# Turning the residual stream of a two-layer decoder: tokens on partitions, 512-column moving weights, norms along rows

## The reference, cut to what matters

```python
for layer in range(2):
    mixer = even_mixer if layer == 0 else odd_mixer      # mLSTM + pooling, or gated linear attention
    x = x + mixer(rmsnorm(x, norm[layer]))               # ends in y @ w_out, w_out is (2048, 2048)
    h = rmsnorm(x, f_norm[layer])
    # product-key expert retrieval: 8 heads x 16 of 16384 one-neuron experts
    q = h @ w_q                                          # (2048, 2048), then scores, top-k, softmax g
    a = h . u_tab[expert]                                # first table, 16384 x 2048
    x = x + sum(g * gelu(a) * v_tab[expert])             # second table, 16384 x 2048
out = rmsnorm(x, final_norm)

def rmsnorm(x, g):
    return x * rsqrt(mean(x * x, axis=-1) + 1e-6) * g    # mean over the 2048 channels of a token
```

## Time and profile before

| | us |
|---|---|
| median of 3 runs | 4150.47 (4147.67 to 4150.59) |
| the profiled execution, its own time | 4150.45 |
| its span, first to last instruction | 4148.7 |
| PE busy | 4056.4 (98% of the span) |
| PE weight loads (PEld) busy | 3989.7 (96%) |
| DVE busy | 2624.9 (63%) |
| ACT busy | 1848.2 (45%) |
| POOL busy | 146.1 (4%) |
| mean granted TensorE clock | 0.989 of 2.4 GHz |
| DMA | 705.65 MB, mean 170 GB/s |

### The profile page before, as it was taken

The page is one execution under the profiler, slowest core; times in us unless marked ns, Lnnn a source line. Parts: engine busy times, 40 slices in busy tenths (PEclk is TensorE's granted clock), DMA queues, the critical chain, the costliest instruction groups (busy, mean ns, idle before and its releaser), DMA issues.

```text
span 4148.7 us, 90161 instructions
## 1 busy us (share of the span) xinstructions
PE 4056.4 (98%) x34860; PEld 3989.7 (96%) x34860; DVE 2624.9 (63%) x4001; ACT 1848.2 (45%) x2326; POOL 146.1 (4%) x142
## 2 busy tenths in 40 slices
PE   8999999999999999999899999999999999999998
PEld 7999999999999999999898889999999999999998
DVE  4555678778549955444545553887787479655444
ACT  4344444444544444444444444444444544444443
POOL 1111000000000000000003020000000000000000
PEclk9999999999999999999998999999999999999999
DMA  5455565655554555555543456556555654565554
GB/s 177 146 156 169 177 182 182 182 165 157 173 171 157 159 187 190 182 182 182 159 153 118 145 165 185 178 182 182 176 157 162 182 162 157 164 200 182 182 182 152
DMA packets 193647, 705.65 MB, mean 170 GB/s; under 512 B 21808, under 2 KB 22000, under 8 KB 193184
## 3 DMA queue, kind: packets, MB, share of 16 engines
q1 hardware_dynamic: 190224, 692.21, 54.3%
q0 software_dynamic: 3344, 12.32, 0.8%
HBM read 698.16 MB, written 6.29 MB: 170 GB/s over the span
## 4 chain that ended last, share of the span: by engine, by line
PE 92%; DVE 4%; DMA 2%; ACT 1%; issue 1%; POOL 0%; SPq 0%; DVEq 0%; POOLq 0%; ACTq 0%
PE ps L1422 29%; PE ps L1423 28%; PE ps L1424 28%; PE ps L1775 2%; DMA w_raw<-in_dense 1%; DVE w_lo L926 1%; DVE big L986 1%; DMA w_raw<-in_v_tab 1%; ACT w_hi L493 1%; PE ps L1683 0%; PE ps L1684 0%; PE ps L1685 0%; PE ps L1629 0%; DVE act_lo_t L975 0%; PE ps L1731 0%
## 5 line engine op out<-in xcount | busy, mean ns | idle before, releaser
L1422 PE MATMUL ps<-act_lo_t,w_hi 128*128 128x256 f32 x10112 | 2902.7, 287 | 46.2 <-DVE act_lo_t L975 35.3
L1423 PE MATMUL ps<-act_hi_t,w_lo 128*128 128x256 f32 x10112 | 2870.4, 284 | 0.0
L1424 PE MATMUL ps<-act_hi_t,w_hi 128*128 128x256 f32 x10112 | 2869.3, 284 | 0.0
L926 DVE TENSOR_TENSOR w_lo<-w_raw,w_hi 128x1024 fp32r<-128x1024 f32 x1312 | 1619.4, 1235 | 1392.6 <-ACT w_hi L493 1379.2
L493 ACT ACTIVATE w_hi<-w_raw 128x1024 fp32r<-128x1024 f32 x1312 | 1388.7, 1059 | 1727.5 <-DMA w_raw<-in_v_tab 888.7
L1422 PEld LDWEIGHTS ps<-act_lo_t,w_hi 128*128 128x128 f32 x10112 | 1948.4, 193 | 57.5 <-issue 40.3
L1423 PEld LDWEIGHTS ps<-act_hi_t,w_lo 128*128 128x128 f32 x10112 | 1950.7, 193 | 0.1
L1424 PEld LDWEIGHTS ps<-act_hi_t,w_hi 128*128 128x128 f32 x10112 | 1949.1, 193 | 0.0
L846 ACT ACTIVATE big<-ps 128x256 f32 (+1 forms) x256 | 98.6, 385 | 282.8 <-PE ps L1424 282.4
L1309 DVE TENSOR_TENSOR big<-big,ps 128x512 f32 (+1 forms) x128 | 171.2, 1339 | 8.4 <-PE ps L1775 8.4
L1369 DVE TENSOR_TENSOR act_lo_t<-big,act_hi_t 128x256 fp32r<-128x256 f32 x384 | 160.3, 419 | 0.0
(11 more groups left out here) (219 smaller groups left out, 1341.4 us busy)
## 6 DMA issues: line engine op xcount, KB each, us to landing
w_raw<-in_u SPq DMA_DIRECT2D x512, 512.0 KB, 3.5
w_raw<-in_v_tab SPq DMA_DIRECT2D x512, 512.0 KB, 3.7
w_raw<-in_dense SPq DMA_DIRECT2D x288, 512.0 KB, 3.6
x_spill<-big POOLq DMA_DIRECT2D x16, 256.0 KB, 4.8
big<-x_spill POOLq DMA_DIRECT2D x16, 256.0 KB, 4.5
big<-in_xT SPq DMA_DIRECT2D x4, 512.0 KB, 5.5
big<-in_keys POOLq DMA_DIRECT2D x2, 1024.0 KB, 11.1
out<-big SPq DMA_DIRECT2D x4, 512.0 KB, 2.7
```

What stands on the lines that cost most here:

```text
L926: dve.tensor_tensor(w_lo[:, slot, :], w_raw[:, slot, :], w_hi[:, slot, :].bitcast(F32), ALU.subtract).then_inc(s_lo, 1)
L1422: pe.matmul(out, wh, xl, start=start, stop=False, **kw)
L1423: pe.matmul(out, wl, xh, start=False, stop=False, **kw)
L1424: return pe.matmul(out, wh, xh, start=False, stop=stop, **kw)
```

## The change

The residual lies with tokens on partitions: two blocks (tb) of 128 tokens x 2048 channels. The output projections and the second table are computed in the form of the value projections (activation stationary, 512 weight columns moving). Of the host's layouts, `w_out` is cut by groups of 512 columns and `x`, the result and the last gain come by rows. A norm becomes: ACT squares a row piece with a sum along the row (`square`), DVE adds four sums, ACT the root, DVE the reciprocal (`deviation`); PE multiplies the residual by a diagonal matrix of these reciprocals, which turns it back to channels on partitions and scales it in one (`turn`); ACT and DVE make `act_hi_t` and `act_lo_t` from PSUM with the gain as scale (`turned_hi`, `turned_lo`). POOL adds the two parts to get `h` where the small gate projections need it (`whole`). The last slabs of `out` and `vt` are taken token block by token block, so that the first block's norm can start under the second's matmuls. The last norm needs no turning. `spread` reads PSUM with a step and writes runs of eight tokens.

```diff
+            def whole(fill):
+                for c in range(CHUNKS):
+                    pool.wait_ge(s_alo, KB * fill + 2 * c + 2)
+                    pool.tensor_tensor(at(HT + 512 * c, 512, 2), act_hi_t[:, 2 * c:2 * c + 2, :].bitcast(F32),
+                                       act_lo_t[:, 2 * c:2 * c + 2, :].bitcast(F32), ALU.add).then_inc(s_h, 1)
...
+                if layer == 1:
+                    pool.wait_ge(s_used, SLAB0["vt", 1] + 2 * HALF + RING)
+                    pool.dma_start(at(F_GAIN, D), last_gain).then_inc(s_last_gain, 16)
...
+            def square(k, n):
+                tb, c = ROWS[k][n]
+                if k == 0:
+                    act.wait_ge(s_x[2 * tb + c // 2], 16)
+                else:
+                    act.wait_ge(s_xadd, rows_added(k, n + 1))
+                i = 4 * tb + c
+                act.activation(at(HT + 512 * i, 512), xs(tb, c), ACT.Square,
+                               accum_out=ssq[:, i:i + 1]).then_inc(s_square, 1)
+            def deviation(k, tb):
+                act.wait_ge(s_msum, TB * k + tb + 1)
+                act.activation(root[:, tb:tb + 1], msum[:, tb:tb + 1], ACT.Sqrt, bias=epst[:, 0:1],
+                               scale=1.0 / D).then_inc(s_root, 1)
+            def deviations(k, n0=0):
+                for n in range(n0, FIRST_DONE[k]):
+                    square(k, n)
+                deviation(k, 0)
+                for n in range(FIRST_DONE[k], 8):
+                    square(k, n)
+                deviation(k, 1)
+            def turned_hi(k):
+                for j in range(KB):
+                    if j % 4 == 0:
+                        act.wait_ge(s_turned, TB * KB * k + KB + j + 4)
+                    act.activation(act_hi_t[:, j, :].rearrange("p (b t) -> p b t", b=TB), turned(j), ACT.Copy,
+                                   scale=gain[:, G_NORM[k] + j:G_NORM[k] + j + 1]).then_inc(s_ahi, 1)
+            def norm(k, n0):
+                hi(0, n0)
+                hi(1, n0 + 1)
+                turned_hi(k)
+                hi(2, n0 + 2)
+                hi(3, n0 + 3)
...
+                for s in range(RING, 32):
+                    lo(s % RING, n0 + s)
+                    if s % 8 == 3:
+                        g = s // 8 - 1
+                        dve.wait_ge(s_used, n0 + 8 * g + 8)
+                        for tb in range(TB):
+                            dve.tensor_tensor(xs(tb, g), xs(tb, g), bank(OUT_BANKS[layer][g % 2][tb]),
+                                              ALU.add).then_inc(s_xadd, 1)
+                k = 2 * layer + 1
+                for tb in range(TB):
+                    if tb == 0:
+                        dve.wait_ge(s_ypart, 4 * layer + 1)
+                    else:
+                        dve.wait_ge(s_used, n0 + 32)
+                    dve.tensor_tensor(xs(tb, 3), xs(tb, 3), bank(OUT_BANKS[layer][1][tb]), ALU.add).then_inc(s_xadd, 1)
+                    deviation(k, tb)
+            def deviation(k, tb):
+                dve.wait_ge(s_square, 8 * k + (8 if tb else FIRST_DONE[k]))
+                dve.tensor_reduce(msum[:, tb:tb + 1], ssq[:, 4 * tb:4 * tb + 4], AX.X, ALU.add).then_inc(s_msum, 1)
+                dve.wait_ge(s_root, TB * k + tb + 1)
+                ins = dve.reciprocal(rroot[:, tb:tb + 1], root[:, tb:tb + 1])
+                if k == 4:
+                    ins.then_inc(s_diag, 1)
+                else:
+                    chain(ins)
+                    dve.tensor_scalar(diag[:, tb, :], ident[:, :], rroot[:, tb:tb + 1], None, ALU.mult).then_inc(s_diag, 1)
+            def turned_lo(k, fill):
+                for j in range(KB):
+                    if j % 4 == 0:
+                        dve.wait_ge(s_ahi, KB * fill + j + 4)
+                    dve.scalar_tensor_tensor(out=act_lo_t[:, j, :].rearrange("p (b t) -> p b t", b=TB), in0=turned(j),
+                                             scalar=gain[:, G_NORM[k] + j:G_NORM[k] + j + 1],
+                                             in1=act_hi_t[:, j, :].bitcast(F32).rearrange("p (b t) -> p b t", b=TB),
+                                             op0=ALU.mult, op1=ALU.subtract).then_inc(s_alo, 1)
...
-                    grid = at(HALF * T * part, HALF * T).rearrange("p (e t) -> p t e", t=T)
+                    grid = at(HALF * T * part, HALF * T).rearrange("p (e t) -> p e t", t=T)
-                    dst = grid[:, t0:t0 + 8, :] if isinstance(i, int) else grid[:, bass.ds(t0, 8), :]
-                    dve.tensor_tensor(dst, dst, bank(4 + k, 512, 8), ALU.mult).then_inc(s_g, 1)
+                    dst = grid[:, :, t0:t0 + 8] if isinstance(i, int) else grid[:, :, bass.ds(t0, 8)]
+                    dve.tensor_tensor(dst, dst, bank(4 + k).rearrange("p (t e) -> p e t", t=8),
+                                      ALU.mult).then_inc(s_g, 1)
...
+                def add(n):
+                    tb, c = BY_BANK[n]
+                    if c < 2:
+                        dve.wait_ge(s_used, vbase + 2 * N_KEYS - RING)
+                    elif n < 7:
+                        dve.wait_ge(s_ypart, 4 * layer + 1 + (n - 4) + 1)
+                    else:
+                        dve.wait_ge(s_used, vbase + 2 * N_KEYS)
+                    dve.tensor_tensor(xs(tb, c), xs(tb, c), bank(2 * c + tb),
+                                      ALU.add).then_inc(s_xadd, 1)
+                for n in range(4):
+                    add(n)
+                if layer == 1:
+                    dve.wait_ge(s_last_gain, 16)
+                    dve.wait_ge(s_xadd, rows_added(k, 4))
+                    for c in range(2):
+                        dve.tensor_tensor(at(F_SCALED + 512 * c, 512), xs(1, c), at(F_GAIN + 512 * c, 512),
+                                          ALU.mult).then_inc(s_scaled, 1)
+                for n in range(4, 6):
+                    add(n)
+                deviation(k, 0)
+                def finished(tb, c):
+                    dve.scalar_tensor_tensor(out=at(F_OUT + D * tb + 512 * c, 512), in0=xs(tb, c),
+                                             scalar=rroot[:, tb:tb + 1], in1=at(F_GAIN + 512 * c, 512),
+                                             op0=ALU.mult, op1=ALU.mult).then_inc(s_fin, 1)
+                if layer == 1:
+                    dve.wait_ge(s_diag, TB * k + 1)
+                    finished(0, 0)
+                    finished(0, 1)
+                add(6)
+                add(7)
+                if layer == 1:
+                    finished(0, 2)
+                    finished(0, 3)
+                deviation(k, 1)
+                if layer == 1:
+                    dve.wait_ge(s_diag, TB * k + 2)
+                    finished(1, 2)
+                    finished(1, 3)
...
+            def turn(k):
+                for tb in range(TB):
+                    pe.wait_ge(s_diag, TB * k + tb + 1)
+                    for j in range(KB):
+                        pe.matmul(ps[:, j // 4 * 2 + tb, P * (j % 4):P * (j % 4 + 1)],
+                                  at(XT + D * tb + P * j, P), diag[:, tb, :], start=True, stop=True).then_inc(s_turned, 1)
+            def out_gemm(layer, beside):
+                n0 = SLAB0["out", layer]
+                def piece(g, q, tb):
+                    for k in range(2):
+                        kb = 2 * q + k
+                        if g == 0 and tb == 0:
+                            pe.wait_ge(s_alo, KB * FILL["y", layer] + kb + 1)
+                        c = slice(512 * k, 512 * (k + 1))
+                        t = slice(P * tb, P * (tb + 1))
+                        o = bank(OUT_BANKS[layer][g % 2][tb])
+                        pe.matmul(o, act_lo_t[:, kb, t], w_hi[:, q % 4, c], start=kb == 0, stop=False)
+                        pe.matmul(o, act_hi_t[:, kb, t], w_lo[:, q % 4, c], start=False, stop=False)
+                        ins = pe.matmul(o, act_hi_t[:, kb, t], w_hi[:, q % 4, c], start=False, stop=kb == KB - 1)
+                    return ins
+                for g in range(4):
+                    if g >= 2:
+                        pe.wait_ge(s_xadd, rows_added(2 * layer + 1, 2 * (g - 1)))
+                    for q in range(8 if g < 3 else 4):
+                        pe.wait_ge(s_lo, n0 + 8 * g + q + 1)
+                        piece(g, q, 0)
+                        piece(g, q, 1).then_inc(s_used, 1)
+                        if g == 0 and q in beside:
+                            beside[q]()
+                for q in range(4, 8):
+                    pe.wait_ge(s_lo, n0 + 24 + q + 1)
+                    ins = piece(3, q, 0)
+                ins.then_inc(s_ypart, 1)
+                for q in range(4, 8):
+                    piece(3, q, 1).then_inc(s_used, 1)
+                turn(2 * layer + 1)
...
+                    for tb in range(TB):
+                        for n in range(2):
+                            ins = v_piece(s, half, buf, tb, n)
                     ins.then_inc(s_used, 1)
+                def v_piece(s, half, buf, tb, n):
```

(24 more changed lines are left out.)

293 lines of the change are left out of this document (103 added, 190 removed).

## The result

| | before | after |
|---|---|---|
| median of 4 runs each | 4149.07 (4146.87 to 4150.59) | 4050.49 (4048.42 to 4051.30) |
| the profiled execution | 4150.45 | 4048.42 |
| its span | 4148.7 | 4046.7 |
| mean granted TensorE clock | 0.989 | 0.992 |

The ratio is 0.9767, with a 95% interval from 0.9755 to 0.9778: 98.6 us less by the medians, 102.0 by the two profiled executions, against 110 forecast. The time lies in the range given, 4028 to 4062.

The account below looks back on a forecast made before the run. The prediction took PE, busy 98% of the span, as the bound. Its terms 92 + 4 + 3 + 5 + 5 = 109 us less, rounded to 110, gave 4040 us from 4150.45, range 4028 to 4062.

Parts of the forecast that it names:

- matmul form, 576 slabs: Output projections and second table: a slab goes from 2.88 to 2.72 us, 92 us less.
- norms 1 and 3: After the output projections: 4.2 us saved, a new wait of 2.3 against it, 4 us less for both.
- norm 2: After the second table: 37.0 us become 33.6, with a PE wait of 6.4 us, 3 us less.
- the end: After the last table, to the span's end: 32.1 us become 27.0, 5 us less.
- the start: Program start: the second block begins at 32 instead of 37.08, 5 us less, between 4 and 7.
- layer 1's `out`, opening: One wait of about 6 us replaces several short ones; about even, up to 3 us either way.
- would take 3.16: Second-table slabs beside `scatter`: PE's time for a slab falls from 3.32 to 3.16 us.
- The ring: Supply of weight slabs: three slabs at the new pace are 8.16 us, leaving 1.7 us of slack of 2.2.
- `spread`: DVE beside `scatter`: 1.0 us taken, bounds 0.69 and twice the present length; rival that it becomes the bound, chance 0.03.
- the prediction's own formula: DVE beside `scatter` in the second table: with a `spread` of X us it needs 2.48 + X/2 a slab.
- the boundaries: Rival: the reordered norms, start and end give nothing or lose; 4058, up to 4068 us; chance 0.13.
- The 512 form: Rival: 512-column matmuls don't keep their pace in the table, the ring holding slabs at 2.88 us; 4123 us; chance 0.04.

Follow-up runs that it names:

- the tail experiments: Two runs, tail_staggered and tail_plain, that changed the order of the table's last four slabs in the changed kernel: 4041.49 and 4049.11 us.
- half_moving: The changed kernel with each 512-column matmul of the second table split into two of 256: 4116.36 us, ratio 0.9921 to the kernel before.
- no_low_part: The changed kernel without the second table's matmuls with `w_lo`, part of the computation missing: 3874.12 us, a single execution.
- tail_plain: The changed kernel with each table's last four slabs in the order of all others, no token block early: 4049.11 us, ratio 0.9766.
- combined: The changed kernel with tail_staggered's order, layer 1's `out` opening reordered on ScalarE and VectorE, and the last gain fetched in eight pieces: 4033.25 us, ratio 0.9723.
- before_warm: The kernel before, with 40 unread matmuls of ones put between the first norm's sum and the first projection: 4145.16 us, ratio 0.9997.
- tail_staggered: The changed kernel with each table's last four slabs begun as they arrive: 4041.49 us, ratio 0.9744 to the kernel before.

## Why the prediction was right, and where it was not

| step | forecast, us less | measured in the two profiles |
|---|---|---|
| matmul form, 576 slabs | 92 | 88: 448 x 0.16 + 128 x 0.127 |
| norms 1 and 3 | 4 | 3.7 |
| norm 2 | 3 | 2.9 |
| the end | 5 | 4.9 |
| the start | 5 | 8.2 |
| layer 1's `out`, opening | 0, up to 3 either way | -4.0 |

Norms 1 and 3 are 29.7 and 29.5 us before, 27.2 and 27.1 after, counted as in the table of the tail experiments, and 0.6 of each difference belongs to the form. The last row is layer 1's `out` up to its last four slabs, 90.0 us before and 89.5 after: 0.5 less, where the form alone takes off 28 x 0.16 = 4.5. The rows add to 103.7; four slabs each of norm 2 and the end are in two of them, 1.3 us, which leaves 102.4, against 102.0 between the two profiled executions. The forecast had the same double count. That it closes so well is partly chance. The tables' parts beside `scatter` are 19.4 us shorter, where the form gives 16.3, and the slabs between them and the last four 57.6 shorter, where it gives 60.2. Both have stalls that come and go: before, one slab at half clock at 1234 us (2.6 us) and one at 3572 (2.4); after, three of 0.75 beside the reload of x and the 2.0 behind the gain's transfer.

- **The matmul form** carried the forecast, and half_moving shows it for what it is: at the full clock 0.013 us for each matmul with its weight load, at 256 columns and at 512. The Trainium skill ("TensorE: Matmul & The Clock Gate", Back-to-back issue gap) gives 2.5 ns for the gap of an isolated matmul, by which the change would bring an estimated 17 us, and it says that beside weight loads this is too little for few columns and too much for 512. The trace does not agree: it has 13 ns at 512 columns too. The step that was off is "would take 3.16" beside `scatter`. The measured slab is 3.20, 4 us in all, and why the switch between the two forms of matmul takes 0.48 us now and took 0.45 is open.
- **The ring**: "1.7 us are left of 2.2" was wrong, though it decided nothing. A single latency over three slabs, 2.13 us, isn't the pace of a supply whose transfers slow each other: with PE out of the way a slab came in 2.39 us, so three slabs had some 1.0 us to spare.
- **`spread`** was right in that it does not bound, at 0.68 us even shorter than the value taken. By the prediction's own formula VectorE then needs 2.48 + 0.34 = 2.82 us a slab, and no_low_part has 2.78. "2.4 ns an element" for the old form is a slip: 1.34 us for 512 elements are 2.6 ns. PE's wait for the last `spread` of a part gave back 1.1 us (2.7 to 1.6), as forecast.
- **Norm 2 and the end** came out within 0.5 and 0.2 us (34.1 for 33.6, 27.2 for 27.0), with steps that partly cancel. The waits were 6.2 and 6.1 us for 6.4, the four slabs with their half clock 13.2 and 12.9 for 13.2, and what follows 14.7 for 14.0 at norm 2 and 8.1 for 7.4 at the end. The copies took 5.93 to 5.95 us for 16, against 0.36 each. What the forecast did not ask is whether the wait was worth its lead; tail_plain says that it was not.
- **The start**: "the second slab's `w_hi` ends at 20.86 whatever the norm does" failed. It ends at 18.47, its load having landed 2.4 us sooner, and the copies of the tiles begin at 18.93. The first block takes 6.6 us, at full clock. In twelve profiles with the new start its first matmul stands anywhere from 21.0 to 24.8, and the second block from 27.5 to 31.4, so against the 37.08 before this term is worth 6 to 9.5 us. In the latest of them (combined) that `w_hi` ends at 20.85, as before the change: when the loads of the start land is a matter of the execution, and the 5 us forecast are the low end. That the clock has no part in the gain is shown by before_warm.
- **Layer 1's `out`** is the term that was mis-sized, 4.0 us where at most 3 were allowed. The wait was forecast (6 us, measured 5.7), but called even with the short ones before. What was left out is that it is one long wait, and the granted clock is halved for the next 6.3 us: 15 matmuls at 0.43 us in place of 0.23, 3 us more. In the kernel before no slab of this opening starts more than 2.6 us late, and the clock stays at full.

Of the rivals, the boundaries neither gave nothing nor lost: they gave 14 us, the double count taken out. The 512 form kept its pace, with some 0.3 us to spare. `spread` did not become the bound. By the medians the gain is 3.4 us smaller than by the profiled executions, of which that of before stands 1.4 us above its median and that of after 2.1 below.

## What to carry to other kernels

Where TensorE never waits, count its matmuls: here, at the full clock, each with its weight load costs 13 ns beside its columns, and half as many, twice as long, gave 2.72 for 2.88 us. When a pass is reordered so that one half is ready early, let it start on what has arrived; a wait for all of the last tiles gave back all that the lead was worth. And before a slow clock is blamed for a slow stretch, look at who is waited for in it: if it is another engine, a faster clock ends nothing sooner.

## What was not expected of the hardware

- A product that reads PSUM in steps of 64 words (128x512 elements, `spread`) takes 0.68 us, as long as one that reads it in a row; the same product with the steps in both of its SBUF streams and PSUM contiguous takes 1.34.
- ScalarE's square with a sum along the row is two instructions in the trace. The sum's own, in the changed kernel's timeline, stands behind each:

```profile
1947.03 0.63 ACT L616 ACTIVATE big<-big 128x512 f32<-128x512 f32 x1 [1.89 <-DVE big L1459]
1947.57 0.19 ACT L616 ACTIVATION_READ_ACCUMULATOR big<-big 128x1 f32 x1
```

- With the granted clock at 1.2 GHz a matmul of 512 columns starts every 0.427 us, against 0.227 at 2.4, so the 13 ns are gone. The half clock stood behind waits of 5.7 and 6.1 us, and not behind one of 1.23 us in tail_staggered. But it also stood behind two of 0.9 and 1.2 us at 1232 to 1234 us in the kernel before, where between them PE had only eight matmuls of two columns.
- A load of 512 KB lands 3.5 us after its issue in the changed kernel and 4.5 us in the stretch at 219 GB/s, and there a ring of four slots fed one slab in 2.39 us, slower than the 2.13 that its latency of 6.4 us over three slabs would let one think.
